# Neighbourhood attention on two key blocks a query tile, and the modulation in four column groups

## The reference

```python
mod = jax.nn.silu(c) @ w_ada + b_ada                  # c: one row a request group
shift, scale, gate = jnp.split(mod, 3, axis=-1)
h = rms_norm(x, ln_g) * (1.0 + scale[:, None, :]) + shift[:, None, :]
# A: differential attention, 4 heads of 2 x 64, rope, all keys
# B: neighbourhood attention, 8 heads of 64, grid of rows x 64 columns
#    window of 8 rows x 16 columns, clipped at the edges, plus a bias rpb by offset
# C: dilated attention, 3 groups x 4 heads of 128, rope, outputs mixed by denominators
for i, y_i in enumerate((ya, yb, yc)):
    u = jax.nn.sigmoid(g_i) * ((y_i * jax.nn.silu(z_i)) @ w_br[i])
out = merged @ w_out                                   # merged: the sum of the u
return x + gate[:, None, :] * out
```

## Time and profile before

| | us |
|---|---|
| median of 3 runs | 2624.71 (2624.29 to 2624.86) |
| profiled execution | 2624.21 |
| its span | 2622.4 |
| PE busy | 2529.2 (96%) |
| DVE busy | 1466.3 (56%) |
| ACT busy | 1040.7 (40%) |
| POOL busy | 154.6 (6%) |

### The profile page before, as it was taken

One profiled execution on the slowest core, in us unless ns is written; L12 is line 12 of the kernel. 1 busy time (PEld: TensorE's weight loads), 2 busy tenths in 40 slices (PEclk: granted clock), 3 DMA queues, 4 the chain that ended last, 5 costly groups with the idle time before them and its releaser, 6 DMA issues.

```text
span 2622.4 us, 39336 instructions
## 1 busy us (share of the span) xinstructions
PE 2529.2 (96%) x14945; PEld 2234.1 (85%) x14945; DVE 1466.3 (56%) x4017; ACT 1040.7 (40%) x2688; POOL 154.6 (6%) x140
## 2 busy tenths in 40 slices
PE   4899999999999999999989999999999999999999
PEld 0687888889889999978878888888988999997888
DVE  1777523677535766643458773277753566764432
ACT  2555622444314444332235663145441344443220
POOL 1200000231000000000010000033100000000000
PEclk9999999999999999999999999999999999999999
DMA  6012122110221111122240102111121111112213
GB/s 251 37 61 72 42 72 72 61 58 17 77 72 38 49 49 49 73 88 72 69 142 25 56 26 80 61 44 36 44 65 62 60 49 40 59 73 69 73 57 117
DMA packets 38810, 171.55 MB, mean 65 GB/s; under 512 B 4704, under 2 KB 9568, under 8 KB 36704
## 3 DMA queue, kind: packets, MB, share of 16 engines
q1 hardware_dynamic: 26352, 147.34, 16.2%
q10 hardware_dynamic: 12272, 21.71, 2.5%
HBM read 162.74 MB, written 6.29 MB: 64 GB/s over the span
## 4 chain that ended last, share of the span: by engine, by line
PE 90%; DVE 4%; ACT 3%; ACTq 2%; issue 1%; DVEq 0%
PE ps_proj L504 70%; PE ps_pv L589 6%; PE ps_pt L574 3%; PE ps_score L560 3%; PE ps_proj L655 2%; PE ps_score L556 2%; PE ps_tr L605 1%; PE ps_tr L606 1%; PE ps_tr L597 1%; DVE normed L1034 1%; DVE top L1117 1%; PE ps_score L524 1%; PE ps_proj L524 1%; DVE act_lo L1025 0%; ACT probs L827 0%
## 5 line engine op out<-in xcount | busy, mean ns | idle before, releaser
L504 PE MATMUL ps_proj<-w_hi,act_hi 128*128 128x384 f32 x1920 | 668.1, 348 | 24.5 <-POOL act_lo L484 15.2
L504 PE MATMUL ps_proj<-w_hi,act_lo 128*128 128x384 f32 x1920 | 647.1, 337 | 0.0
L504 PE MATMUL ps_proj<-w_lo,act_hi 128*128 128x384 f32 x1920 | 647.0, 337 | 0.0
L504 PE MATMUL ps_proj<-act_hi,w_hi 128*128 128x512 f32 (+1 forms) x1408 | 477.7, 339 | 12.0 <-DVE act_lo L1253 6.1
L504 PE MATMUL ps_proj<-act_lo,w_hi 128*128 128x512 f32 (+1 forms) x1408 | 475.4, 338 | 0.0
L504 PE MATMUL ps_proj<-act_hi,w_lo 128*128 128x512 f32 (+1 forms) x1408 | 474.4, 337 | 0.0
L504 PEld LDWEIGHTS ps_proj<-w_hi,act_hi 128*128 128x128 f32 x1920 | 363.7, 189 | 30.4 <-issue 20.4
L504 PEld LDWEIGHTS ps_proj<-w_lo,act_hi 128*128 128x128 f32 x1920 | 364.1, 190 | 0.0
L504 PEld LDWEIGHTS ps_proj<-w_hi,act_lo 128*128 128x128 f32 x1920 | 363.0, 189 | 0.0
L504 PEld LDWEIGHTS ps_proj<-act_hi,w_hi 128*128 128x128 f32 x1408 | 268.0, 190 | 43.7 <-issue 7.8
L504 PEld LDWEIGHTS ps_proj<-act_hi,w_lo 128*128 128x128 f32 x1408 | 267.8, 190 | 28.7
(11 more groups left out here) (136 smaller groups left out, 3428.8 us busy)
## 6 DMA issues: line engine op xcount, KB each, us to landing
w_raw<-in_w SPq DMA_DIRECT2D x128, 768.0 KB, 4.4
w_raw<-in_w SPq DMA_DIRECT2D x40, 512.0 KB, 3.6
w_ada<-in_w_mod SPq DMA_DIRECT2D x11, 1536.0 KB, 6.3
first_ada<-in_w_first SPq DMA_DIRECT2D x4, 2048.0 KB, 14.5
out_y<-merged ACTq DMA_DIRECT2D x16, 384.0 KB, 4.6
merged<-in_x_in ACTq DMA_DIRECT2D x8, 384.0 KB, 28.8
x_old<-in_x_in ACTq DMA_DIRECT2D x8, 384.0 KB, 5.1
x_old<-out_y ACTq DMA_DIRECT2D x8, 384.0 KB, 5.2
```

Of the source, the lines that this page charges most:

```text
L504: op = pe.matmul(out, sta[s](k), mov[m](k), start=(k == 0 and n == 0), stop=(k == chunks - 1 and n == 2))
```

## The change

**Mixer B's prompt.** The order of the tokens inside a prompt tile becomes a permutation (`_quarter`), the same for all. For mixer B the projections read the activations of tile t at columns t, t + 4, t + 8 and so on (`tokens`), so that a tile of keys holds 16 neighbouring columns of the grid in all eight rows. A tile of queries then needs two tiles of keys: t and t + 1 for t < 3, and 0 and 3 for the last (`near_blocks`). For that the turned queries are spread over the tiles as ACT copies them out, in an instruction of their own, and the turned results go back to the common order. Tile, mask and bias shapes shrink to 256 keys, DVE's share of the copy goes away in B, and three of the four prompt tiles have the same biases, so POOL makes them in four parts a head. The relative biases of the prompt come in eight DMAs a head, no longer two, and for heads 1 to 3 behind tile 1 of the head before.

**Modulation.** `c_silu` goes into a stationary operand 32 columns wide, zeros behind the two (`c_wide`). The eight chunks go into four groups of 32 columns of the array, two chunks each, with outputs in partitions 0, 32, 64 and 96 on (`columns_of`). ACT copies all 128 partitions, and the turn becomes an f32 matmul with `sums`, which adds the four partial rows. `between(1)` of an `a` unit comes behind all its matmuls.

The diff, cut to its core (the masks, tallies and shape arguments that follow from it are left out):

```diff
         rel_p = sb("rel_p", [P, 2, RP], F32, slot2)
-        rel_s = sb("rel_s", [P, 2, RS], F32, slot2 + 4 * 2 * 288)
-        bias = [sb(f"bias{b}", [P, 2, 512], F32, slot2 + 4 * (2 * (288 + 160) + 1024 * b)) for b in range(2)]
-        assert 2 * (288 + 160) + 2048 <= 3 * TOK + 9 * P
+        rel_s = sb("rel_s", [P, 2, RS], F32, slot2 + 4 * 2 * 256)
+        bias = [sb(f"bias{b}", [P, 2, 256], F32, slot2 + 4 * (2 * (256 + 160) + 512 * b)) for b in range(4)]
+        assert 2 * (256 + 160) + 2048 <= 3 * TOK + 9 * P
         probs = [sb(f"probs{b}", [P, 1024]) for b in range(2)]
         row_lam = sb("row_lam", [P, 256], F32, t_at["probs0"])
-        probs_t = sb("probs_t", [P, 1024])
+        probs_t = sb("probs_t", [P, 768])
         square = sb("square", [P, 256])
...
-        mb_bits = sb("mask_b_sb", [P, TILES, 64], U16)
+        mb_bits = sb("mask_b_sb", [P, 3, 64], U16)
+        c_wide = sb("c_wide", [P, KC, 32])
+        sums = sb("sums", [P, 2])
...
+        def keys_of(kind, t):
+            return 256 if kind == "B" else GROUPS[group_of(t)][2]
+        def near_blocks(t):
+            return (t, t + 1) if t < 3 else (0, 3)
+        def bias_part(t):
+            return 0 if t < 3 else t - 2
         def blocks(kind, t):
             if kind == "B":
-                return [(m * 512 + b * P, 0, g0 + b, slice(64 * m, 64 * m + 64), slice(64 * m, 64 * m + 64))
-                        for m in range(2) for b in range(n)]
+                tiles = near_blocks(t) if t < 4 else (4, 5)
+                return [(m * 512 + b * P, 0, vt, slice(64 * m, 64 * m + 64), slice(64 * m, 64 * m + 64))
+                        for m in range(2) for b, vt in enumerate(tiles)]
             return ([(b * P, 0, g0 + b, slice(0, P), slice(0, P)) for b in range(n)]
...
-            def biases(a):
-                l, _, h, t = a
-                if t == 0:
-                    pool.wait_ge(*rel_p_in.at((l, h)))
-                if t == 4:
-                    pool.wait_ge(*rel_s_in.at((l, h)))
-                n = ATT_AT[a]
-                if (l, h, t) not in ((l, 0, 0), (l, 0, 1)):
-                    pool.wait_ge(*masked.at(ATT[n - 2]))
-                grp = group_of(t)
-                table, off, rws = (rel_p, RP - 1 - (3 - t), 8) if grp == 0 else (rel_s, RS - 1 - (2 - 2 * (t - 4)), 4)
-                for m in range(2):
-                    v = table[:, m, :]
-                    win = bass.AP(v.tensor, v.offset + off, [v.ap[0], [-1, 4], [-31, rws], [-4, 16]])
-                    mk = mb[:, t, :]
-                    mk = bass.AP(mk.tensor, mk.offset, [mk.ap[0], [16, 4], [0, rws], [1, 16]])
-                    out = bias[n % 2][:, m, 0:64 * rws].rearrange("p (r k c) -> p r k c", r=4, k=rws)
-                    op = pool.tensor_tensor(out, win, mk, ALU.add)
-                op.then_inc(*bias_ready.inc(a))
+            def biases(l, h):
+                for part, last in enumerate((2, 3, 4, 5)):
+                    if part == 0:
+                        pool.wait_ge(*rel_p_in.at((l, h)))
+                    if part == 2:
+                        pool.wait_ge(*rel_s_in.at((l, h)))
+                    if h > 0:
+                        pool.wait_ge(*masked.at((l, "B", h - 1, last)))
+                    for m in range(2):
+                        v = (rel_p if part < 2 else rel_s)[:, m, :]
+                        mk = mb[:, 0, 32 * part:32 * part + 32] if part < 2 else mb[:, part - 1, :]
+                        out = bias[part][:, m, :]
+                        if part < 2:
+                            for blk in range(2):
+                                off = RP - 1 - (16 * blk if part == 0 else 8)
+                                win = bass.AP(v.tensor, v.offset + off, [v.ap[0], [-1, 4], [-31, 8], [-4, 4]])
+                                mp = bass.AP(mk.tensor, mk.offset + 16 * blk, [mk.ap[0], [4, 4], [0, 8], [1, 4]])
+                                op = pool.tensor_tensor(
+                                    out[:, blk * P:(blk + 1) * P].rearrange("p (r k c) -> p r k c", r=4, k=8), win, mp,
+                                    ALU.add)
+                        else:
+                            off = RS - 1 - (2 - 2 * (part - 2))
+                            win = bass.AP(v.tensor, v.offset + off, [v.ap[0], [-1, 4], [-31, 4], [-4, 16]])
+                            mp = bass.AP(mk.tensor, mk.offset, [mk.ap[0], [16, 4], [0, 4], [1, 16]])
+                            op = pool.tensor_tensor(out.rearrange("p (r k c) -> p r k c", r=4, k=4), win, mp, ALU.add)
+                    op.then_inc(*bias_ready.inc((l, h, part)))
...
-                    pool.wait_ge(consts_in, 16 * 6)
-                a_next = OPENED[n + 1] if n + 1 < len(UNITS) else None
-                if a_next is not None and a_next[1] == "B":
-                    biases(a_next)
+                    pool.wait_ge(consts_in, 16 * 7)
+                if u[0] == "q" and u[5] == 5 and (u[2] == "B" or u[2:4] == ("A", 3)) and u[2:4] != ("B", 3):
+                    biases(u[1], (u[3] + 1) % HEADS)
...
+            def tokens(a, k, kind, t):
+                if kind != "B" or t >= 4:
+                    return a[:, k, t * P:(t + 1) * P]
+                return a[:, k, t:SEQ:4]
...
+            def columns_of(bank, c0, n, w_):
+                for k in range(KC):
+                    g = 32 * (k % 4)
+                    op = pe.matmul(bank[g:g + 32, c0:c0 + n], c_wide[:, k, :], w_[:, k, :], start=k < 4, stop=k >= 4)
+                return op
-                    bank = (ps_score if i < 2 else ps_proj)[0:2, (i % 2) * 512:(i % 2) * 512 + 512]
-                    for k in range(KC):
-                        op = pe.matmul(bank, c_silu[:, k, :], first_ada[i][:, k, :], start=k == 0, stop=k == KC - 1)
+                    op = columns_of(ps_score if i < 2 else ps_proj, (i % 2) * 512, 512, first_ada[i])
-                pe.wait_ge(consts_in, 16 * 6)
+                pe.wait_ge(consts_in, 16 * 7)
-                    op = pe.transpose(ps_pv[:, 2 * s:2 * s + 2], first_row[0:2, s * P:(s + 1) * P], ident[0:2, 0:2])
+                    op = pe.matmul(ps_pv[:, 2 * s:2 * s + 2], first_row[:, s * P:(s + 1) * P], sums[:],
+                                   start=True, stop=True)
...
-                        op = pe.matmul(ps_score[:, 512 * m:512 * m + keys], qkv[h % 2][rows_, 0, t * P:(t + 1) * P],
-                                       qkv[h % 2][rows_, 1, g0 * P:g0 * P + keys], start=True, stop=True)
+                        q, k = qkv[h % 2][rows_, 0, t * P:(t + 1) * P], qkv[h % 2][rows_, 1, g0 * P:g0 * P + keys]
+                        if kind == "B" and t < 4:
+                            v = qkv[h % 2][rows_, 1, :]
+                            b0, b1 = near_blocks(t)
+                            k = bass.AP(v.tensor, v.offset + b0 * P, [v.ap[0], [(b1 - b0) * P, 2], [1, P]])
+                        op = pe.matmul(ps_score[:, 512 * m:512 * m + keys], q, k, start=True, stop=True)
...
-                        op = pe.transpose(ps_tr[:, 2 * s:2 * s + 2], mod_row[0:2, u[2] % 2, s * P:(s + 1) * P],
-                                          ident[0:2, 0:2])
+                        op = pe.matmul(ps_tr[:, 2 * s:2 * s + 2], mod_row[:, u[2] % 2, s * P:(s + 1) * P], sums[:],
+                                       start=True, stop=True)
-            pe.wait_ge(ones_set, 2)
+            pe.wait_ge(ones_set, 3)
...
-                    sta = [lambda k, a=a: a[:, k, t * P:(t + 1) * P] for a in (act_hi, act_lo)]
+                    sta = [lambda k, a=a: tokens(a, k, kind, t) for a in (act_hi, act_lo)]
-                    for k in range(KC):
-                        op = pe.matmul(ps_proj[0:2, bank:bank + ADA], c_silu[:, k, :], w_ada[b][:, k, :],
-                                       start=k == 0, stop=k == KC - 1)
-                        between(k)
-                    op.then_inc(*proj_ready.inc(u))
+                    columns_of(ps_proj, bank, ADA, w_ada[b]).then_inc(*proj_ready.inc(u))
+                    between(1)
...
-                    act.dma_start(rel_p[:, m, :], bass.AP(src.tensor, src.offset + (rel_base + 3 - RP),
-                                                          [[31, 8], [4, 16], [1, RP]])).then_inc(rel_p_in.sem, 16)
+                    for r in range(4):
+                        act.dma_start(rel_p[32 * r:32 * r + 32, m, :],
+                                      bass.AP(src.tensor, src.offset + (rel_base + 8 + r - RP),
+                                              [[31, 8], [4, 4], [1, RP]])).then_inc(rel_p_in.sem, 16)
...
+                    if kind == "B" and t < 4:
+                        first, step = (((t - 1) * P + 2, P - 2) if t in (1, 2) else (3 * P, -3 * P) if t == 0
+                                       else (2 * P + 2, P))
+                        v = qkv[h % 2][:, 0, :]
+                        act.activation(bass.AP(v.tensor, v.offset + first, [v.ap[0], [4, 32], [step, 2], [1, 2]]),
```

(61 more changed lines are left out.)

26 lines of the change are left out of this document (15 added, 11 removed).

## The result

The changed kernel takes 2577.16 us (median of 4 runs, 2575.82 to 2577.75), the kernel before 2624.76 on the same chip (4 runs, 2624.29 to 2624.86): ratio 0.9815, 95% interval 0.9803 to 0.9827, 47.6 us less. The forecast was 2536, its range 2513 to 2578. The time stands at the upper edge of that range and outside the forecast's own 2515 to 2556. It is near where the first rival put it, strided loads about twice as long, 2574.

What follows compares the result with a forecast made beforehand. The prediction took TensorE (PE), busy 96% of the span, as the bound. Its terms were 56 + 35 + 9 - 9 - 3 = 88 us saved, so 2624.2 - 88 = 2536 us, range 2513 to 2578.

Steps and rivals of the forecast that it cites:

- the first rival: Mixer B's prompt projections: strided weight loads about twice as long, adding 38 us, so 2574 us; chance 0.17.
- The forecast case: Whole kernel: all terms hold and 88 us are saved, giving 2536 us, own range 2515 to 2556; chance 0.59.
- Part 1, the shapes: Mixer B's prompt tiles on two blocks of keys: 1.76 us less PE work in each of 32, 56.3 us saved.
- The price hidden in part 1: Mixer B's prompt projections: 768 strided weight loads, taken as 0 us because they stay hidden under the matmuls; 38 at most.
- the POOL ratio: POOL's elements at a step of four f32 are 1.28 times as slow as contiguous; applied to PE's weight loads.
- Part 2 in the units: Eleven later modulation units in four column groups: net 3.55 us saved each, less 4 for lost cover, 35 us.
- "pairs" case: Modulation: column groups overlap only by pairs, the sixteen instructions taking about 3 us, so 2551 us; chance 0.13 including no overlap.
- The start: First modulation: PE's block ends sooner, so DVE first uses the modulation 7 to 11 us earlier; 9 taken.
- DMA issues on ACT: More bias DMAs hold ACT's queue: 9 us lost in A's last heads, 3 in the six later heads.
- Column groups without overlap: Modulation: the four column groups do not run at once, so 2590 us; a third of a 0.13 chance shared with pairs.
- ACT's queue as the bound: A's last head and tile 1: issues at 1.1 us each, slow recovery, 15 to 20 us more, 2554 us; chance 0.07.
- slower than before: Mixer B's projections: PE waits for the strided load in all 768 matmuls; 2748 us at four times the load; chance 0.04.

Runs made afterwards that it cites:

- e8_both: The changed kernel with contiguous loads in mixer B, tokens sorted behind the projection, and one DMA a head for each bias table: 2510.15 us.
- e4_step4: The kernel before, with only mixer B's prompt projections reading their stationary activations at a step of four f32: 2671.88 us.
- e3_columns_only: The kernel before with only the modulation in four column groups and its sums, three small start-up tiles in another buffer: 2573.64 us.
- e6_tables: The changed kernel with relative biases laid out per partition in the input, one DMA a head for the prompt and one for the sample: 2557.83 us.
- e5_steps: The kernel before with mixer B's prompt loads at steps of 2, 3, 4 and 6 f32 in its four heads: 2648.88 us, one run.
- e7_shuffle: The changed kernel with contiguous weight loads in mixer B, tokens sorted behind the projection by ACT's copies and DMAs on SP's queue: 2539.52 us.

## Why the prediction missed: step by step

The time lies inside the stated range, 0.8 us below its upper end. The forecast case, with 0.59 of the chance, did not happen: the kernel gained 47.6 us and not 88. By the prediction's own sign (starts 0.2 us apart or more) it was wrong, and in one term. That the range held is partly luck: it kept 38 us for the strided loads, which cost 47, and part 2 of the change happened to bring 7 us more than forecast.

**Part 1, the shapes: right.** 56.3 us forecast. `e8_both`, without the strided loads, has 46.5 less 39.6 = 6.9 us a head against 7.04, and PE has no wait in that head, so ACT and DVE stayed covered. The changed kernel itself shows it in the one stage where mixer B's attention runs beside contiguous projections, B's last head under the first projections of mixer C: 46.53 us before, 39.52 after, in both layers. I had that sum from two rows of shapes that already existed.

**The price hidden in part 1: this is the step that failed.** The prediction said "I take 0, by the POOL ratio" and kept 38 for the range. It is 5.9 us a head (`e4_step4` in head 2, 52.4 against 46.5), 47.2 us for eight; 45.7 measured for `e4_step4` as a whole. The reasoning started from a load of 128 columns at 0.112 us under a matmul of 0.174, and no run speaks against these two. What failed was the row for the ratio between them. The 1.28 came from another engine, whose whole instruction is 512 elements at 1454 ns, 2.8 ns an element. The load takes 0.112 us for 128 columns, 0.9 ns each, and its factor is about 0.23 / 0.112 = 2.1. That so slow an engine has no time to lose where the load has is my reading; no run tests it. The rule of the Trainium skill that the prediction quotes ("SBUF — State Buffer", section "Door 1: The DMA port swizzle") spoke for a penalty, and I gave that case 0.17. Its consequence, worked out there as 38 us from an assumed 0.224 a load, was short by 8 to 9, since the spacing is 0.233 and not 0.224.

**Part 2 in the units: right in mechanism, short in size.** 35 us forecast. `e3_columns_only` has 52.5 less about 9 for the start, so 43; the lengths of the stages give about 42. The sixteen take 1.50 us (1.6 forecast), and the six passes of the sums 0.73 (0.65). The 4 us set aside for the lost cover were not needed: an `a` unit shortened its head by 3.6 us in A's second and third head, as the sum had it, and in `e3_columns_only` by 4.0 in B's two and 5.5 in A's last. The starts of the sixteen in an `a` unit come in fours, 6 to 7 ns apart in a four and 0.32 to 0.35 us from four to four (436.617, .623, .630, .637, then 436.963). So both the "pairs" case and the one without overlap are out.

**The start: right.** 9 us forecast; from the start of the span to the first projection it is 78.4 before and 69.4 after.

**DMA issues on ACT.** A's last heads: 9 us forecast, 2.8 in layer 0 (51.43 us against 48.60 in `e3_columns_only`, which has the `a` unit's gain) and 3.8 in layer 1, so 6.7. B's heads: 3 forecast, about 3.6 against `e3_columns_only` less the net 1.1 a head; `e6_tables` takes back 2.9 of it. The twelve issues take 8.9 us from the first to the last one's end, and part of PE's idle time was there before. In layer 1 more than half of the price is not the wait itself but the lower clock behind it, which the prediction left out.

**Sum.** -56.3 + 47.2 - 9.0 - 42 + 6.7 + 3.6 = -49.8 against -47.5 in the two spans. Of the 2 us left, 1.7 lie in the first head of A in each layer, which is longer than before; why was not followed up. Had the strided load stood in the sum with its measured price, the forecast would have been 2583, 6 us above the result.

**Rivals.** Strided loads twice as long, 2574 with chance 0.17: what happened. Column groups without overlap, ACT's queue as the bound, and slower than before did not. `e5_steps` bears on the slow rival, which needed a load of 0.29 us: from step 4 to step 6 the price did not grow beyond 0.233.

## What to carry to other kernels

When a change alters how a matmul's stationary operand is laid out, put the load's own time beside the matmul's. Here a load of 128 columns had 60 ns to spare under its matmul, and a step of four f32 made it about 120 ns longer. Gather where a copy is made anyway, behind the projection rather than in its load. And count the DMA issues on a compute engine's queue before you tune the work in front of them, since a shorter unit uncovers what a longer one hid: `e6_tables` and `e7_shuffle` together gave 9.8 us more than the sum of the two.

## What the runs showed of the hardware

- A load of 128 f32 columns under matmuls of 384: starts 0.174 us apart at steps of 1 and 2 elements, 0.178 at 3, 0.233 at 4, 0.230 at 6 (`e5_steps`). The load's own row: 188, 195, 255, 330 and 327 ns.
- Four column groups of 32 run at once: 16 instructions (eight f32 matmuls) of 384 columns in 1.50 us, 3.5 times as fast as one after the other (5.32). The fourth group took part like the rest.
- After 6.50 us idle, PE ran at the lower clock (0.32 us from start to start) for 3.7 us of matmuls before it was back at 0.174. The length of the idle time alone does not tell: in the same unit of A's last head, `e3_columns_only` ran at the lower clock after 2.52 us idle in layer 0 (0.32 us apart), and the kernel before at the full clock after 2.75 us in layer 1.
- One DMA issue with rows read at three strides held ACT's queue for 681 ns at the median, 1296 at most; those of the kernel before, of the same kind, 625. One issue of `e6_tables`, which reads a table laid out by partition, held it for 335. On ACT's queue, the kernel after, then `e6_tables` (duration ns min/median/max, first and last start):

```profile
L756 ACTq DMA_DIRECT2D rel_p<-in_rpb x64: 680/681/1296, 187.3 to 1785.1; - x64
L752 ACTq DMA_DIRECT2D rel_p<-in_rel_pt x8: 334/335/346, 185.9 to 1759.3; - x8
```
